# Spacing the split weight parts 96 bytes further apart in SBUF

## The reference, cut to what matters

```python
h = rms_norm(x, gain)                      # 256 (or 512) x 1024
u = h @ w_in                               # 1024 x 2866, later 2816 and 3072
x = x + mixed @ w_out                      # 1024 x 1024
x = x + relu(rms_norm(x, gain2) @ w_up)**2 @ w_down   # 1024 x 4096, 4096 x 1024
```

## Time and profile before

| | |
|---|---|
| time, median of three runs | 1114.17 us (1113.1 to 1114.39) |
| span of the profiled execution | 1111.5 us |
| mean granted TensorE clock | 0.996 |
| PE (matmuls) busy | 1070.4 us, 96% |
| PEld (weight loads, beside the matmuls) | 919.4 us, 83% |
| DVE busy | 750.0 us, 67% |
| ACT busy | 548.5 us, 49% |
| DMA, mean | 165 GB/s |

### The profile page before, as it was taken

One profiled execution on the slowest core, in us unless ns is written; L12 is line 12 of the kernel. 1 busy time (PEld: TensorE's weight loads), 2 busy tenths in 40 slices (PEclk: granted clock), 3 DMA queues, 4 the chain that ended last, 5 costly groups with the idle time before them and its releaser, 6 DMA issues. The chain is left out here.

```text
span 1111.5 us, 17674 instructions
## 1 busy us (share of the span) xinstructions
PE 1070.4 (96%) x6914; PEld 919.4 (83%) x6914; DVE 750.0 (67%) x1441; ACT 548.5 (49%) x987; POOL 62.8 (6%) x79
## 2 busy tenths in 40 slices
PE   8999999999999999999999999999998899999986
PEld 6877879899987887889989998798876587989855
DVE  5765756655556566785888878789866945834475
ACT  5543845444444543854444444534546834523273
POOL 1000001000000000000000000100211301000000
PEclk9999999999999999999999999999999999999998
DMA  9768055565555558035855655763247033844100
GB/s 332 256 210 315 2 157 185 173 206 190 189 170 178 189 184 312 30 119 190 179 180 194 198 185 182 245 226 105 85 142 257 2 114 133 224 136 146 22 19 40
DMA packets 55335, 183.35 MB, mean 165 GB/s; under 512 B 21076, under 2 KB 33748, under 8 KB 35796
## 3 DMA queue, kind: packets, MB, share of 16 engines
q1 hardware_dynamic: 55252, 182.22, 49.9%
HBM read 179.31 MB, written 2.90 MB: 164 GB/s over the span
## 5 line engine op out<-in xcount | busy, mean ns | idle before, releaser
L237 DVE TENSOR_TENSOR w_lo<-ring,w_hi 128x1024 fp32r<-128x1024 f32 x260 | 317.5, 1224 | 197.7 <-ACT w_hi L231 192.9
L231 ACT CAST w_hi<-ring 128x1024 fp32r<-128x1024 f32 x260 | 271.7, 1052 | 322.7 <-PE banks L293 321.3
L293 PE MATMUL banks<-shared_hi,w_hi 128*128 128x256 f32 (+1 forms) x448 | 134.4, 300 | 1.5 <-DVE w_lo L237 1.5
L293 PE MATMUL banks<-shared_lo,w_hi 128*128 128x256 f32 (+1 forms) x448 | 133.9, 299 | 0.0
L293 PE MATMUL banks<-shared_hi,w_lo 128*128 128x256 f32 (+1 forms) x448 | 133.8, 299 | 0.0
L293 PE MATMUL banks<-w_hi,u_hi 128*128 128x512 f32 x256 | 100.2, 391 | 0.2
L293 PE MATMUL banks<-w_lo,u_hi 128*128 128x512 f32 x256 | 100.0, 391 | 0.0
L293 PE MATMUL banks<-w_hi,u_lo 128*128 128x512 f32 x256 | 99.9, 390 | 0.0
L293 PEld LDWEIGHTS banks<-shared_hi,w_hi 128*128 128x128 f32 x448 | 85.8, 192 | 4.2 <-issue 1.7
L293 PEld LDWEIGHTS banks<-shared_hi,w_lo 128*128 128x128 f32 x448 | 85.8, 191 | 2.6
L293 PEld LDWEIGHTS banks<-shared_lo,w_hi 128*128 128x128 f32 x448 | 85.8, 192 | 2.4
(11 more groups left out here) (407 smaller groups left out, 2228.3 us busy)
## 6 DMA issues: line engine op xcount, KB each, us to landing
ring<-in_w_up SPq DMA_DIRECT2D x32, 1024.0 KB, 5.1
ring<-in_w_down SPq DMA_DIRECT2D x32, 1024.0 KB, 5.1
ring<-in_w_in SPq DMA_DIRECT2D x23, 1024.0 KB, 5.2
ring<-in_ab_ada SPq DMA_DIRECT2D x12, 1024.0 KB, 5.1
ring<-in_cd_ada SPq DMA_DIRECT2D x12, 1024.0 KB, 5.0
ring<-in_cd_in SPq DMA_DIRECT2D x12, 1024.0 KB, 5.5
ring<-in_w_out SPq DMA_DIRECT2D x8, 1024.0 KB, 7.1
ring<-in_ab_in SPq DMA_DIRECT2D x16, 512.0 KB, 5.1
```

Of the source, the lines that this page charges most:

```text
L231: nc.scalar.copy(w_hi[:, n % PARTS, :], part_source(key, q)).then_inc(hi_ready, 1)
L237: nc.vector.tensor_tensor(w_lo[:, n % PARTS, :], part_source(key, q), w_hi[:, n % PARTS, :].bitcast(F32), ALU.subtract).then_inc(part_read ...
L293: mm = nc.tensor.matmul(dst, a, b, start=first_one and i == 0, stop=last_one and i == 2, skip_group_check=shares_bank)
```

## The change

The pitch of the parts in `w_hi` and `w_lo` grows from 1024 to 1048 elements, by 96 bytes. The two tiles are allocated with the larger pitch, and a view cuts each part to its 1024 elements, so every instruction keeps its shape and only start addresses differ. A filler of 192 bytes behind them completes the growth to 768 bytes (twice 288, and 192), six times 128, so each later tile keeps its place modulo 128 bytes.

```diff
 PIECES = 4
+PITCH = PART + 24
 PIECE = PART // PIECES
...
         ring = sbuf("ring", [P, SLOTS, HALF])
-        w_hi, w_lo = sbuf("w_hi", [P, PARTS, PART], F32R), sbuf("w_lo", [P, PARTS, PART], F32R)
+        w_hi, w_lo = (sbuf(n, [P, PARTS, PITCH], F32R)[:, :, 0:PART] for n in ("w_hi", "w_lo"))
+        sbuf("to_line_w", [P, 48])
         x = sbuf("x", [P, 4, D])
```

## The result

The changed kernel takes 1122.58 us (median of 8 runs, 1121.4 to 1129.38); the kernel before takes 1114.28 us in the 8 runs beside it. The ratio is 1.0081, with a 95% interval of 1.0057 to 1.0104: 0.8% slower, +8.3 us by the medians. The forecast was +3.4 us, in the right direction and too small by more than half; the time lies just above the forecast's own range (to 1122.2) and inside the outer one (to 1123.0). The span of the profiled execution is 1120.0 us, 8.5 more than before.

What follows compares the result with a forecast made beforehand. The prediction took TensorE's matmul pace at L293 as the bound. Stationary loads +5.76 us and moving weights -2.35 us gave +3.4 us, 1117.6 us; own range 1115.3 to 1122.2, outer range 1109.8 to 1123.0 us.

Steps and rivals of the forecast that it cites:

- The bound: Whole kernel: TensorE sets the time nearly everywhere, through the pace of the 4704 matmuls at L293; PE busy 96%.
- The moving term: Matmuls with weight parts moving: 1408 of 2112 get an operand off the 128-byte line, -1.7 ns each, -2.35 us.
- since the price was the same for both widths on the line, I carry it over: Moving weights: `f`'s -1.7 ns at 256 columns applied to matmuls of 512 or 306 columns.
- its other end: Upper bound for moving weights off the line: +3 ns a matmul, +4.2 us.
- The stationary term: Matmuls with weight parts stationary: 1728 of 2592 loads begin off the 128-byte line, +3.33 ns each, +5.76 us.
- A fifth costs 3.3 ns: Weight load off the line reads five 128-byte stretches instead of four; four cost the exposed 13.3 ns.
- The sum: Whole kernel: +5.76 - 2.35 = +3.4 us, 1117.6 us.
- Relative place decides: Rival: pairs at unequal places modulo 128 gain 1.7 ns a matmul; -3.95 us, 1110.2 us; chance 0.18.
- Nothing happens: Rival: TensorE doesn't notice starts off by multiples of 32 bytes; 1114.2 us; chance 0.17.

Runs made afterwards that it cites:

- e1: Pitch of the weight parts 128 bytes larger, all parts at multiples of 128 bytes, against the kernel before: ratio 1.0061, 1122.23 us.
- e3: All weight parts and activations moved together by 96 bytes, against the kernel before: ratio 1.0012, medians 1117.76 against 1112.82 us.
- e4: Filler before layer 0's `u` removed, so this `u` alone moves to 32 bytes before the weights' place, against the kernel before: ratio 1.0006, 1114.56 us.
- e13: Pitch 256 bytes larger and all weight parts shifted by 192 bytes, against the kernel before: 1119.80 us in one run.
- e10: Pitch 256 bytes larger and all weight parts shifted by 16 bytes, against the kernel before: 1120.90 us in one run.
- e8: Pitch 256 bytes larger and all weight parts shifted by 32 bytes, against the kernel before: 1123.04 us in one run.
- e5: Pitch 256 bytes larger with no shift, every place modulo 256 bytes kept, against the kernel before: ratio 1.0008, medians 1116.34 against 1113.1 us.
- e6: Pitch 256 bytes larger and all weight parts shifted by 128 bytes, against the kernel before: 1131.99 us in one run.
- e7: Pitch 256 bytes larger and all weight parts shifted by 64 bytes, against the kernel before: 1114.67 us in one run.
- e12: Parts placed by use: 0 for 512 columns, 64 bytes behind the moving operand for 256, against the kernel before: 1110.55 against 1113.2 us, ratio 0.9956.

## Why the prediction was right or wrong

**The bound: right.** TensorE's pace on the 4704 matmuls set the time. The line's busy time grew by 7.84 us, the span by 8.5, and ScalarE and VectorE kept their durations: the splits take 1050 and 1223 ns in the stretch of layer 1, as before, and relu, the square and the cast 1020, 1220 and 1050 ns, against the earlier trace rows.

```profile
L239 DVE TENSOR_TENSOR w_lo<-ring,w_hi 128x1024 fp32r<-128x1024 f32 x72 | 88.0, 1223 | 24.5 <-ACT w_hi L233 24.4
L233 ACT CAST w_hi<-ring 128x1024 fp32r<-128x1024 f32 x71 | 73.6, 1050 | 83.2 <-PE banks L295 83.2
L2569 DVE TENSOR_TENSOR square<-relu 128x1024 f32<-128x1024 f32 x8 | 9.8, 1220 | 0.0
L2517 ACT CAST u_hi<-square 128x1024 fp32r<-128x1024 f32 x8 | 8.4, 1050 | 19.6 <-DVE square L2569 19.6
L2515 ACT ACTIVATE relu<-banks 128x1024 f32<-128x1024 f32 x8 | 8.2, 1020 | 0.0
```

**The moving term, -2.35 us: wrong in sign.** This is the step that failed first: "since the price was the same for both widths on the line, I carry it over". In step, the price above the streaming time is indeed the same at both widths. Out of step it isn't: 256 columns gain some 2 ns, 512 columns lose some 5. The 1920 matmuls with 512 columns of moving weights cost +9.5 us, outside even the +4.2 us that I gave as its other end. Under it lay the wrong cause: I took the place of one operand against a 128-byte line for what counts, and e1 (all but `f` on the line, 231.0 ns) and e3 (all off it, 227.1 ns) show that it is the difference of the two places.

**The stationary term, +5.76 us: wrong in kind.** "A fifth costs 3.3 ns", for a fifth stretch of 128 bytes, has no counterpart; that a load is read in such stretches no run shows. e3 puts every stationary operand off the 128-byte line and none slows down; in the changed kernel the 1536 loads under 256 columns of `shared` and `h_cd` go with 2.0 ns less, not more. Only the 288 under 512 columns cost more, 4.4 ns, as the moving ones do. The term measured -1.8 us.

**The sum.** +9.6 (all 2112 moving, unrounded) and -1.8 in the place of -2.35 and +5.76. Both terms had the wrong sign, and the two errors partly cancel: the direction came out right by luck, and the forecast earned nothing by it.

**The rivals.** "Relative place decides" had the mechanism, as e3, e4 and e13 show. It had the wrong period, 128 instead of 256 bytes, and took `f`'s gain for all widths, so it gave -3.95 us. I held that it "wins as soon as stationary parts off the line cost under nothing"; they do cost under nothing at 256 columns, and the kernel is slower all the same, through the width. "Nothing happens", with the Trainium skill's 16-byte lines (SBUF — State Buffer, Specifications) beside it, fell: with e10 16 bytes of difference, a whole such line, already change 226.9 to 231.7 ns. The Trainium skill's rule that the weight load takes no bandwidth from the running matmul (TensorE: Matmul & The Clock Gate, Part 2) doesn't cover what is seen here: the pace of load and stream together depends on the difference of their places, 227 ns in step and 233 at 32 bytes (e8). The float32 rows had nothing to say, since in both products the two operands lay at equal places.

**What could have been seen.** The trace of before had a single row on an uneven pair, at 256 columns, and the names of the fillers spoke of 128-byte lines. I took the modulus from the names; no row supported it against 256.

## What to carry to other kernels

When float32r matmuls with a new weight load each time bound a kernel, keep the two operands' start addresses equal modulo 256 bytes where 512 columns stream, and unequal (here the stationary one 64 bytes behind) where 256 do; moving everything by 96 bytes cost nothing measurable. Why the wide stream loses and the narrow one gains out of step isn't shown, so measure both again elsewhere. Don't carry a placement effect from one width to another, and don't take the modulus from one pair: give every pitch or filler a control that changes the footprint and not the remainder, as e5 did. Read such effects in start times of the timeline, as means over some tens of intervals, which repeat to about half a ns where the time of whole runs scatters by 8 to 10 us.

## What the hardware showed that I had not expected

- The period is 256 bytes: a pitch larger by 128 costs 0.6% (e1), one larger by 256 nothing that shows (e5), and a shift by 128 gives 232.4 ns (e6).
- Paces lock: 120.0, 226.7 and 233.3 ns, and the 113.3 of e7, are 288, 544, 560 and 272 columns' time at 2.4 GHz, that is the streamed columns plus 32, 32, 48 and 16. Other means, such as 118.3, are averages over intervals that vary, 115 to 123 ns for `f` before the change; the 117.7 of e7 and e12 is nearly steady (117 to 119) and no such sum.
- One difference can have two paces in one kernel, 113.3 and 117.7 ns at +64 bytes. What chooses between them stays open, and so does the pair of reads that meet. A way to hold all 256-column products at 113.3 ns wasn't found; it would give (120.0 - 113.3) x 1536 = 10.3 us on those with `shared` and `h_cd` against the kernel before.
